# VectorE's order in the scan, and the bank turns and the y normalisation of the merge stage, in a two-block float32 kernel

## The reference

```python
for l in range(2):
    proj = rms_norm(h, norm1_g[l]) @ w_in[l]
    z, xbc, dt, q, k, v, gates = split(proj)
    xbc = silu(causal_conv(xbc, conv_w, conv_b))        # width 4, 4096 channels
    x, B, C = split(xbc)                                # 2048, 8 x 128, 8 x 128
    y = ssd(x, softplus(dt), a_log, B, C) + x * d_skip  # 32 heads of 64, 8 groups
    y = y * silu(z)
    y = rms_norm_per_group(y, 8 groups of 256) * ssd_norm_g
    o = sliding_window_attention(q, k, v)
    g_ssd, g_attn = split(sigmoid(gates + b_gate))
    h = h + (g_ssd * (y @ w_ssd_down) + g_attn * (o @ w_attn_down)) @ w_o
    h = h + square(relu(rms_norm(h, norm2_g) @ w_mlp_up)) @ w_mlp_down
return h[16:]
```

## Time and profile before

| | |
|---|---|
| median of three runs | 3000.49 us (2998.08 to 3002.07) |
| the profiled execution | 3002.07 us, span 3000.8 us |
| TensorE busy | 2936.9 us, 98% |
| VectorE, ScalarE, GpSimd busy | 64%, 49%, 36% |
| DMA queue of the weights | 47.0% of 16 engines' time, 453.32 MB |
| scan, layers 0 and 1 | 1904 to 2059 us, 2534 to 2687 us |
| merge up to g0, layers 0 and 1 | 2059 to 2097 us, 2687 to 2723 us |

### The profile page before, as it was taken

The page is one execution under the profiler, slowest core; times in us unless marked ns, Lnnn a source line. Parts: engine busy times, 40 slices in busy tenths (PEclk is TensorE's granted clock), DMA queues, the critical chain, the costliest instruction groups (busy, mean ns, idle before and its releaser), DMA issues.

```text
span 3000.8 us, 49383 instructions
## 1 busy us (share of the span) xinstructions
PE 2936.9 (98%) x20180; PEld 2601.4 (87%) x20180; DVE 1922.7 (64%) x3336; ACT 1467.9 (49%) x2491; POOL 1080.4 (36%) x462
## 2 busy tenths in 40 slices
PE   7999999998999999999999999999999999999999
PEld 5878887786788886599999987889999988899999
DVE  2777775666576655667655456677466666775676
ACT  3453332444443323665555446665464456664553
POOL 0423223000322222045535532343555533444554
PEclk9999999999999999999999999999999999999999
DMA  7556653211257752058735533344555433445554
GB/s 235 201 168 197 196 193 116 71 57 43 87 194 252 252 177 64 29 183 275 239 95 184 188 115 101 112 119 141 177 169 183 155 120 110 117 126 183 183 185 139
DMA packets 404560, 459.89 MB, mean 153 GB/s; under 512 B 8688, under 2 KB 381424, under 8 KB 404336
## 3 DMA queue, kind: packets, MB, share of 16 engines
q1 hardware_dynamic: 401248, 453.32, 47.0%
q10 hardware_dynamic: 3088, 3.42, 0.4%
HBM read 455.66 MB, written 1.05 MB: 152 GB/s over the span
## 4 chain that ended last, share of the span: by engine, by line
PE 90%; DVE 6%; ACT 2%; issue 1%; DMA 1%; ACTq 0%; DVEq 0%
PE bank L445 25%; PE bank L447 24%; PE bank L446 24%; PE banks L445 1%; PE banks L447 1%; PE banks L446 1%; PE bank L1485 1%; DVE wl L405 1%; PE banks L1496 1%; PE banks L2701 1%; DMA X<-in_ctxT 1%; PE banks L1833 1%; PE banks L1822 1%; PE bank L1812 1%; PE bank L1815 1%
## 5 line engine op out<-in xcount | busy, mean ns | idle before, releaser
L420 POOL TENSOR_TENSOR wl<-raw,wh 128x768 fp32r<-128x768 f32 (+3 forms) x324 | 926.9, 2861 | 1682.8 <-ACT wh L386 1682.8
L386 ACT ACTIVATE wh<-raw 128x2048 fp32r<-128x2048 f32 (+1 forms) x336 | 636.1, 1894 | 474.5 <-PE bank L447 387.9
L405 DVE TENSOR_TENSOR wl<-raw,wh 128x1280 fp32r<-128x1280 f32 (+3 forms) x332 | 512.8, 1545 | 345.6 <-ACT wh L386 345.4
L445 PE MATMUL bank<-nh,wh 128*128 128x272 f32 (+1 forms) x1712 | 502.6, 294 | 4.7 <-DVE y L2439 3.3
L447 PE MATMUL bank<-nh,wl 128*128 128x272 f32 (+1 forms) x1712 | 491.6, 287 | 0.0
L446 PE MATMUL bank<-nl,wh 128*128 128x272 f32 (+1 forms) x1712 | 489.7, 286 | 0.0
L445 PE MATMUL bank<-xh,wh 128*128 128x512 f32 (+2 forms) x1282 | 440.9, 344 | 4.1 <-DVE xl L801 3.7
L447 PE MATMUL bank<-xh,wl 128*128 128x512 f32 (+2 forms) x1282 | 433.9, 338 | 0.0
L446 PE MATMUL bank<-xl,wh 128*128 128x512 f32 (+2 forms) x1282 | 433.6, 338 | 0.0
L445 PE MATMUL bank<-hh,wh 128*128 128x512 f32 (+1 forms) x1024 | 344.1, 336 | 0.0
L446 PE MATMUL bank<-hl,wh 128*128 128x512 f32 (+1 forms) x1024 | 344.1, 336 | 0.0
(11 more groups left out here) (493 smaller groups left out, 5661.9 us busy)
## 6 DMA issues: line engine op xcount, KB each, us to landing
raw<-in_mlp_w SPq DMA_DIRECT2D x128, 1024.0 KB, 5.7
raw<-in_w_in SPq DMA_DIRECT2D x60, 1024.0 KB, 5.2
raw<-in_mod_wT SPq DMA_DIRECT2D x48, 1024.0 KB, 5.1
extra<-in_mod_wT SPq DMA_DIRECT2D x36, 1024.0 KB, 5.6
raw<-in_w_mlp_up SPq DMA_DIRECT2D x32, 1024.0 KB, 5.4
raw<-in_w_mlp_down SPq DMA_DIRECT2D x32, 1024.0 KB, 5.0
raw<-in_w_in SPq DMA_DIRECT2D x34, 512.0 KB, 4.8
raw<-in_w_ssd_down SPq DMA_DIRECT2D x16, 1024.0 KB, 5.0
```

Source lines behind the costliest of these rows:

```text
L386: nc.scalar.activation(self.wtile(self.wh, c1), self.rawtile(c1), AF.Copy).then_inc(*up("act_wh", ("wh", c1)))
L405: nc.vector.tensor_tensor(l, r, h.bitcast(F32), ALU.subtract).then_inc(*up("dve_wl", ("wl_dve", c1), *([("wl_pool", c1)] if n == self.P[c1 ...
L420: nc.gpsimd.tensor_tensor(l, r, h.bitcast(F32), ALU.subtract).then_inc(*up("pool_wl", ("wl_pool", c1), *([] if n else [("wl_dve", c1)])))
L445: nc.tensor.matmul(o, ah, bh, start=first, stop=False)
```

## The change

Three edits, all in the second block:
- dve_ssd: in periods 0 to 7 dve_split stands ahead of dve_conv and dve_silu in its step, and in period 8 ahead of dve_skip; dve_weigh and dve_skip change places in the text.
- pe_merge: for j = 1 both g1 and ad groups take their banks from (0, 1, 3); before it was (0, 1) for g1 and (4, 5) for ad. For j = 2, 3 it stays RING.
- y normalisation: pe_ynorm, act_ynorm and dve_ynorm take two groups (four tiles k) in one call. TensorE issues two spread matmuls after both groups of a chunk instead of one after each group. VectorE's unit is multiply, then by turns multiply and subtract, and a last subtract, complete in itself; before, each call did two multiplies and the two subtracts of the call ahead of it. On VectorE a unit now stands behind the split of its chunk and before the two dve_gated of the ad groups; on ScalarE the unit of j = 2's spreads after g1 stands behind act_split of the ad chunk.

```diff
         for g in range(9):
             for i in range(4):
                 if g < 8:
+                    if i % 2 == 0:
+                        self.dve_split(self.ix["x" if i == 0 else "bc", l, g])
                     self.dve_conv(l, g, i)
                 n = 4 * g + i - 1
                 if 0 <= n < 32:
                     self.dve_silu(l, n // 4, n % 4)
-                if g and i >= 2:
-                    self.dve_skip(l, 2 * (g - 1) + i - 2)
-                if i % 2 == 0:
-                    self.dve_split(self.ix["x" if i == 0 else "bc", l, g] if g < 8 else self.ix["g1" if i == 0 else "ad", l, 0])
-                if g and i == 1:
-                    for u in range(4):
-                        self.dve_weigh(l, 4 * (g - 1) + u)
+                if g == 8 and i % 2 == 0:
+                    self.dve_split(self.ix["g1" if i == 0 else "ad", l, 0])
+                if g:
+                    if i == 1:
+                        for u in range(4):
+                            self.dve_weigh(l, 4 * (g - 1) + u)
+                    if i >= 2:
+                        self.dve_skip(l, 2 * (g - 1) + i - 2)
...
                 for m in range(2):
-                    self.pe_group(c, m, slot, src, T, (name, l, 2 * j + m), m == 1, of=RING if j > 1 else (0, 1) if name == "g1" else (4, 5))
-                    if j > 1:
-                        self.pe_ynorm(l, 4 * (j - 2) + (0 if name == "g1" else 2) + m)
+                    self.pe_group(c, m, slot, src, T, (name, l, 2 * j + m), m == 1, of=(0, 1, 3) if j == 1 else RING)
                 if j == 1 and name == "g1":
                     self.pe_pick(l, 7)
+                if j > 1:
+                    self.pe_ynorm(l, 4 * (j - 2) + (0 if name == "g1" else 2))
...
-        for k in (2 * g, 2 * g + 1):
-            if k < 16:
-                DVE.wait_ge(*at("acc", "yn", l, g))
+        for k in range(2 * g0, 2 * g0 + 5):
+            if k < 2 * g0 + 4:
+                DVE.wait_ge(*at("acc", "yn", l, k // 2))
                 if k >= 4:
                     DVE.wait_ge(*at("ynl", l, k - 4))
...
-        for k in (2 * g - 2, 2 * g - 1):
-            if k >= 0:
-                DVE.wait_ge(*at("ynh", l, k))
...
+            if k > 2 * g0:
+                DVE.wait_ge(*at("ynh", l, k - 1))
...
     def act_merge(self, l):
...
         for j in range(1, 4):
             self.act_split(self.ix["g1", l, j])
+            if j == 3:
+                self.act_ynorm(l, 2)
             for m in range(2):
                 self.act_gate(l, "g1", 8, 2 * j + m)
-                if j > 1:
-                    self.act_ynorm(l, 4 * (j - 2) + m)
             self.act_split(self.ix["ad", l, j])
             if j > 1:
-                for m in range(2):
-                    self.act_ynorm(l, 4 * (j - 2) + 2 + m)
+                self.act_ynorm(l, 0 if j == 2 else 4)
+        self.act_ynorm(l, 6)
...
     def dve_merge(self, l):
...
-        self.dve_split(self.ix["g1", l, 1])
-        self.dve_var(f"y{l}", self.place["tot", f"y{l}"][0:8, T], self.rv[0:8, T], 256)
-        self.dve_bits_root(f"y{l}", self.rs[0:8, T], self.rtt[0:8, T], self.rv[0:8, T])
-        self.dve_root_parts(f"y{l}", 8, T)
-        self.dve_split(self.ix["ad", l, 1])
-        for m in range(2):
-            self.dve_gated(l, 2 + m)
-        for j in (2, 3):
-            g = 4 * (j - 2)
-            self.dve_ynorm(l, g)
-            self.dve_ynorm(l, g + 1)
+        for j in range(1, 4):
             self.dve_split(self.ix["g1", l, j])
-            self.dve_ynorm(l, g + 2)
+            if j == 3:
+                self.dve_ynorm(l, 2)
+            if j == 1:
+                self.dve_var(f"y{l}", self.place["tot", f"y{l}"][0:8, T], self.rv[0:8, T], 256)
+                self.dve_bits_root(f"y{l}", self.rs[0:8, T], self.rtt[0:8, T], self.rv[0:8, T])
+                self.dve_root_parts(f"y{l}", 8, T)
             self.dve_split(self.ix["ad", l, j])
-            self.dve_gated(l, 2 * j)
-            self.dve_ynorm(l, g + 3)
-            self.dve_gated(l, 2 * j + 1)
-        self.dve_ynorm(l, 8)
+            if j > 1:
+                self.dve_ynorm(l, 0 if j == 2 else 4)
+            for m in range(2):
+                self.dve_gated(l, 2 * j + m)
+        self.dve_ynorm(l, 6)
```

More of the change, by code:

```diff
@@ L2916, in pe_merge, with pe_ynorm, act_ynorm, dve_ynorm @@
             self.pe_total("n11", T)
-    def pe_ynorm(self, l, g):
+    def pe_ynorm(self, l, g0):
         nc, at, up, PE = self.nc, self.T.at, self.T.up, self.PE
         T = REAL[l]
[L2921 to L2926, removed]
+        for g in (g0, g0 + 1):
+            b = self.pe_bank((6, 7), "yn", l, g)
+            PE.wait_ge(*at("rsp", f"y{l}"))
+            nc.tensor.matmul(b[:, T], self.eye[:, g:g + 1].broadcast_to([128, 128]), self.rsp[:, T], start=True, stop=True
+                             ).then_inc(*up("pe_spread", ("acc", "yn", l, g)))
+    def act_ynorm(self, l, g0):
         nc, at, up, ACT = self.nc, self.T.at, self.T.up, self.ACT
         T = REAL[l]
-        for k in (2 * g, 2 * g + 1):
+        for k in range(2 * g0, 2 * g0 + 4):
             ACT.wait_ge(*at("ynt", l, k))
             nc.scalar.activation(self.yh[:, k, T], self.u[k % 4][:, T], AF.Copy).then_inc(*up("act_ynh", ("ynh", l, k)))
-    def dve_ynorm(self, l, g):
+    def dve_ynorm(self, l, g0):
         nc, at, up, DVE = self.nc, self.T.at, self.T.up, self.DVE
         T = REAL[l]
-        for k in (2 * g, 2 * g + 1):
-            if k < 16:
-                DVE.wait_ge(*at("acc", "yn", l, g))
+        for k in range(2 * g0, 2 * g0 + 5):
+            if k < 2 * g0 + 4:
+                DVE.wait_ge(*at("acc", "yn", l, k // 2))
                 if k >= 4:
@@ L2942, in dve_ynorm @@
                 nc.vector.scalar_tensor_tensor(out=self.u[k % 4][:, T], in0=self.y[:, k, T], scalar=self.col("ssd_g", 16 * l + k),
-                                               in1=self.place["yn", l, g][:, T], op0=ALU.mult, op1=ALU.mult
-                                               ).then_inc(*up("dve_ynt", ("ynt", l, k), ("out", "yn", l, g)))
-        for k in (2 * g - 2, 2 * g - 1):
-            if k >= 0:
-                DVE.wait_ge(*at("ynh", l, k))
-                nc.vector.tensor_tensor(self.yl[:, k, T], self.u[k % 4][:, T], self.yh.bitcast(F32)[:, k, T], ALU.subtract
-                                        ).then_inc(*up("dve_ynl", ("ynl", l, k)))
+                                               in1=self.place["yn", l, k // 2][:, T], op0=ALU.mult, op1=ALU.mult
+                                               ).then_inc(*up("dve_ynt", ("ynt", l, k), ("out", "yn", l, k // 2)))
+            if k > 2 * g0:
+                DVE.wait_ge(*at("ynh", l, k - 1))
+                nc.vector.tensor_tensor(self.yl[:, k - 1, T], self.u[(k - 1) % 4][:, T], self.yh.bitcast(F32)[:, k - 1, T], ALU.subtract
+                                        ).then_inc(*up("dve_ynl", ("ynl", l, k - 1)))
     def act_merge(self, l):
```

## The result

The changed kernel takes 3022.93 us (median of four, 3021.44 to 3026.7) against 3000.4 us: ratio 1.0078, 95% interval [1.006, 1.0095]. It is 22.5 us slower. Forecast were 3012.8 us and 3005 to 3017: the sign was right, the size was not.

The account below looks back on a forecast made before the run. The prediction took TensorE, busy for 98% of the span, to bound the kernel. Its terms 0.4 + 3.0 + 7.2 + 1.7 = 12.3 us gave a median of about 3012.8 us, range 3005 to 3017.

Parts of the forecast that it names:

- What bounds the kernel: Claim that TensorE is busy throughout the edited stretches, so the edits can remove no wait, only make new ones.
- Part 1, the scan: Moving VectorE's split ahead of the convolution delays TensorE 0.2 us per layer, 0.4 us in all.
- the sentence on the later periods: In the scan's later periods, 1.90 us of VectorE idle before the convolution holds the moved subtraction, so nothing is late.
- The small wait expected in step 0: In the scan's first full period GpSimd is pushed back, the SiLU multiply ends later, and TensorE is 0.2 us late.
- The rival of the lost race: In the scan GpSimd starts before VectorE and holds the port: 4 us instead of 0.4, 3016.4 us; chance 0.08.
- Part 2, banks: Bank turns in the merge cost nothing in layer 0, waits of 0.55 and 2.46 us in layer 1: 3.0 us.
- Part 3: Y normalisation in fours returns the spreads' banks late: 3.2 us in layer 0, 4.0 in layer 1, together 7.2 us.
- w to w: Y normalisation chain, from one ScalarE wh start to the next: 7.0 us, or 7.8 with two gates in the last half.
- The exclusive port: In the y normalisation, VectorE's first subtract stands until GpSimd's wl ends, because their shared port pair is locked.
- The clock, one fall: One clock fall after a new merge wait, costing 1.7 us; the ends were 0 and 5.1 us.
- The cover behind the last half: After the y normalisation's last half, the third g0 chunk is split 2.8 us (layer 1: 1.9 us) before it is wanted.
- The sum: All terms together slow the whole kernel by 12.3 us, to a median of about 3012.8 us.

Follow-up runs that it names:

- e9: Kernel before, with VectorE's split ahead of the convolution in step 0 of every period and in step 2 of period 0 alone: 3000.71 us, 1.0001.
- e12: e10 with the last y normalisation unit behind the split of the third g0 chunk on ScalarE and VectorE: 3000.34 us, 1.0003.
- e1: Kernel before with the scan edit alone (dve_ssd of the changed kernel): 3013.77 us, 1.0043.
- e4: Kernel before, with VectorE's split ahead of dve_skip in step 2 of periods 0 to 7, convolution and SiLU product in place: 3019.68 us, 1.0062.
- e5: Kernel before with the scan edit, and dve_skip ahead of the SiLU product in step 2 of periods 1 to 7: 3006.56 us, 1.0025.
- e3: Kernel before with the split ahead of the convolution in step 0 alone (x chunks): 3005.6 us, 1.0018.
- e7: Kernel before with the y normalisation in fours alone, banks and scan as before: 3006.97 us, 1.0028.
- e8: e7 with VectorE's share of the wl subtraction 7/8 instead of 5/8 for ad 3, g0 0 and g0 1: 3005.3 us, 1.0022.
- e10: e7 with the spreads in banks 4 to 7 in turn instead of 6 and 7: 3001.8 us, 1.0008.
- e2: The changed kernel with dve_ssd as before, so bank turns and y normalisation alone: 3011.0 us, 1.0035.
- e6: Kernel before with the bank turns (0, 1, 3) for j = 1 alone: 3002.37 us, 1.001.
- e11: e9's scan and e10's merge in one kernel, with the old bank turns: 3003.49 us, 1.0015.

## Why the prediction was wrong

- **What bounds the kernel: right.** There was nothing to win in these stretches, and the new waits of TensorE are paid: 23.0 us of delay in the four stretches of the table, 22.5 in the median. e9 and e12, which keep most of the new order without its waits, are level with the kernel before.
- **Part 1, the scan, 0.4 us: wrong; 11.35 us by the traces, 13.6 by e1.** The step that failed is the sentence on the later periods, "where the moved subtraction fits ... so nothing is late". It was reckoned with the 1.90 us of idle time ahead of the convolution in step 0, and for the SiLU product alone. In step 2 VectorE's idle 1.46 us ahead of the convolution do not hold the 1.4 us subtraction, since 1.00 of them pass before wh is there. The convolution, the SiLU product and dve_skip all move back by about 1 us, and dve_skip frees the only bank of the state matmuls, with 0.24 us to spare. The prediction looked at dve_skip's place against the weighing only, not against the split, and worked out no bank's slack in the scan. e4 and e5 show that dve_skip decides, in both directions: its delay alone makes the wait, and dve_skip 0.4 us sooner takes 0.4 us from it.
- **The small wait expected in step 0: right.** TensorE is 0.16 us late at the first cb product (forecast 0.2), and with two smaller delays beside it some 0.3 us per layer. Of the 11.35 us this is 0.6; the other 10.7 or so are the state matmuls' waits of step 2. The rival of the lost race did not happen in the changed kernel, but it is real, and near its price: e3 has it in both layers, e5 in one.
- **Part 2, banks, 3.0 us: right.** The marked waits are 0.48 and 2.30 us. By the starts of the matmuls ahead of them, in both kernels, the delays are 0.55 and 2.42, forecast 0.55 and 2.46; layer 0 has none.
- **Part 3, 7.2 us: right.** e7 7.4 us; layer 0's merge adds 3.1 us by the table (forecast 3.2), e7's layer 1 4.0 (forecast 4.0). w to w is 6.98 us (ScalarE's wh at 2079.73 and, in the lines below, at 2086.71), then 7.70 with the two gates, against 7.0 and 7.8.

```profile
2086.71 1.90 ACT L386 ACTIVATE wh<-raw 128x2048 fp32r<-128x2048 f32 x1
...
2094.41 1.91 ACT L386 ACTIVATE wh<-raw 128x2048 fp32r<-128x2048 f32 x1
```

- **The exclusive port.** In e7 the subtract is stretched to 1.10 us, in e8, with GpSimd done sooner, it takes 0.44. Multiplies that read a bank (L2942) run beside GpSimd unstretched, 0.90 for two. The Trainium skill (SBUF — State Buffer, "SBUF: two separate sides") says that of a VectorE instruction with two SBUF inputs and a GpSimd one that reads SBUF the first to start holds the shared port pair to its end. The traces agree: in e3 the 0.69 us subtraction took 3.98 us beside GpSimd's.
- **The clock, one fall, 1.7 us: right for the changed kernel**, after the 2.30 us wait. Its rows had one fall behind two like waits, which leaves none to three open, so that one came is in part luck. The last waits of the layers (1.19 and 1.42), which it counted among the three possible, brought none.
- **The cover behind the last half** was there in the changed kernel, but only because TensorE was late already (e10). It held because the waits before the spreads came.
- **The sum.** With 11.35 instead of 0.4 for the scan, 12.3 us become 23.3; measured were 22.5. So the size missed by one term, the scan.

## What to carry to other kernels

Where an instruction moves ahead of others on an in-order engine, write down every buffer and bank that each of the passed instructions frees, and the slack of each, for every step of the loop where the move happens; here the one with a single bank and the shortest slack decided, not the one nearest to the moved line. An idle gap ahead of an instruction holds a moved one only from the moment at which its input is there. Turns over a tuple whose length does not divide the number of uses give each pass another assignment, so check each pass. A timeline without a marked wait can still hide a small one, so compare the starts of the same instructions in both kernels too.

## What the runs showed of the hardware that was not expected

- When ScalarE's wh releases VectorE and GpSimd together, VectorE starts 0.04 us ahead and GpSimd pays (4.00 instead of 3.55 us in the scan's first full period). If VectorE comes 0.12 us after GpSimd's start, its subtraction takes 3.98 instead of 0.69 us (e3). A tenth of a microsecond in VectorE's order decides over 3.3 us.
- A TensorE wait of 2.30 us in a merge that was otherwise full was followed by a granted clock of 0.79 over 8 us in all three profiles that have it (changed kernel, e2, e6); after the waits of 0.42 to 1.42 us in the merges (e7), of 1.70 us (e10, e11) and of 1.75 and 1.76 us in the scans (e3, e5) it stayed at 1.00, and the 0.75 us waits that return every 18.8 us cost none either. The length of the wait alone does not decide: ahead of layer 0's scan e9's clock fell to 0.79 over 8 us behind a wait of only 1.28 us, and behind the like waits of about 1.6 us in the second block's two projections the clock fell in layer 0 in every profile, in layer 1 in some (changed kernel, e3) and not in others (before, e7).
